# A transformer layer with a mixture of experts on one NeuronCore: first pair's slots freed in halves, the further block behind the eighth pair, bfloat16 one-hots, and the ninth weight unit behind the first gather

## The reference

```python
x = x + g1 * mix                                  # mix = [pooling | linear attention] @ w_out
h = rms_norm(x) * (1.0 + sc2) + sh2               # (512, 1024)
s = sigmoid(h @ w_router)                         # 32 experts in 4 groups of 8
# best group by the sum of its two best (s + bias); two best experts in it; gw = their s, normalised
for each token, for its two experts e:
    y += gw * ((silu(h @ w1[e]) * (h @ w3[e])) @ w2[e])      # w1, w3: 1024 x 512; w2: 512 x 1024
x = x + g2 * y
return rms_norm(x) * final_g
```

## Time and profile before

| | |
|---|---|
| median of 3 runs | 756.38 us (755.04 to 759.0) |
| the profiled execution, own time | 761.83 us |
| its span | 760.0 us |
| PE busy (matmuls) | 700.8 us, 92% |
| DVE, ACT, POOL busy | 343.1, 174.9, 55.5 us |
| transferred | 259.42 MB, mean 341 GB/s |
| chain that ended last | PE 75%, DMA 16%, DVE 7% |

### The profile page before, as it was taken

One profiled execution on the slowest core, in us unless ns is written; L12 is line 12 of the kernel. 1 busy time (PEld: TensorE's weight loads), 2 busy tenths in 40 slices (PEclk: granted clock), 3 DMA queues, 4 the chain that ended last, 5 costly groups with the idle time before them and its releaser, 6 DMA issues.

```text
span 760.0 us, 9258 instructions
## 1 busy us (share of the span) xinstructions
PE 700.8 (92%) x3822; PEld 388.3 (51%) x3822; DVE 343.1 (45%) x624; ACT 174.9 (23%) x309; POOL 55.5 (7%) x55
## 2 busy tenths in 40 slices
PE   3799999999898799989779999999999999998893
PEld 2578778777687444443424443443443443453442
DVE  3554988698865213323314233333333333332326
ACT  4332376532232020210110101110110110110104
POOL 2007700100000100000000000000000000000000
PEclk9899999999999899999987999999999999999997
DMA  9995353844738389998996999999999999999962
GB/s 337 388 382 202 139 200 132 314 147 206 292 137 347 131 354 427 426 425 326 430 425 281 420 415 427 426 426 426 426 428 427 426 427 428 425 428 427 429 286 110
DMA packets 38922, 259.42 MB, mean 341 GB/s; under 512 B 4126, under 2 KB 4510, under 8 KB 26208
## 3 DMA queue, kind: packets, MB, share of 16 engines
q1 hardware_dynamic: 34416, 250.11, 80.5%
q0 software_dynamic: 2688, 4.88, 1.7%
q10 hardware_dynamic: 1776, 3.84, 1.3%
HBM read 259.20 MB, written 4.19 MB: 347 GB/s over the span
## 4 chain that ended last, share of the span: by engine, by line
PE 75%; DMA 16%; DVE 7%; issue 1%; ACT 1%; SPq 1%; DVEq 0%; POOLq 0%
PE bank L904 26%; PE bank L611 16%; PE bank L913 12%; DMA ring<-in_w 8%; PE bank L921 4%; PE bank L922 3%; DMA ring<-in_w_in 3%; DMA xg_rows<-x_rows,keep 3%; DMA x_rows<-mid 2%; PE bank L878 2%; PE bank L893 2%; PE bank L929 1%; PE bank L896 1%; PE bank L731 1%; PE bank L886 1%
## 5 line engine op out<-in xcount | busy, mean ns | idle before, releaser
L904 PE MATMUL bank<-ring,low 128*64 128x512 f32 x944 | 229.7, 603 | 4.8 <-DMA ring<-in_w 4.0
L904 PEld LDWEIGHTS bank<-ring,low 128*64 128x64 f32 x944 | 74.4, 139 | 127.4 <-issue 127.4
L1678 DVE TENSOR_TENSOR x<-x,bank 128x512 f32<-128x512 f32 x136 | 84.4, 683 | 78.5 <-PE bank L922 76.7
L913 PE MATMUL bank<-ring,low 128*64 128x512 f32 x432 | 115.0, 600 | 0.9 <-DVE x L1678 0.9
L913 PEld LDWEIGHTS bank<-ring,low 128*64 128x64 f32 x432 | 35.6, 138 | 67.5 <-issue 65.9
L1668 DVE SCALAR_TENSOR_TENSOR y_raw<-bank,keep,g2b 128x512 f32<-128x512 f32 x32 | 24.0, 751 | 89.2 <-PE bank L913 89.2
L1735 DVE TENSOR_TENSOR low<-low,bank 128x512 f32<-128x512 f32 x16 | 11.0, 688 | 112.9 <-PE bank L904 112.9
L921 PE MATMUL bank<-y_hi,slot_tok 128*128 128x512 f32 x128 | 53.7, 420 | 0.2 <-DVE y_lo L1673 0.2
L922 PE MATMUL bank<-y_lo,slot_tok 128*128 128x512 f32 x128 | 50.6, 395 | 0.0
L1311 ACT COPY low<-bank 128x512 f32<-128x512 f32 x16 | 9.4, 586 | 173.6 <-PE bank L886 173.6
L1835 POOL DMA_INDIRECT xg_rows<-x_rows,keep x17 | 16.9, 996 | 432.5 <-PE bank L878 400.6
(11 more groups left out here) (248 smaller groups left out, 926.0 us busy)
## 6 DMA issues: line engine op xcount, KB each, us to landing
ring<-in_w SPq DMA_DIRECT2D x88, 2048.0 KB, 18.9
ring<-in_w_mod SPq DMA_DIRECT2D x11, 2048.0 KB, 12.3
mid<-in_w SPq DMA_DIRECT2D x11, 2048.0 KB, 17.9
ring<-in_w_in SPq DMA_DIRECT2D x4, 2048.0 KB, 21.7
ring<-in_w_out SPq DMA_DIRECT2D x2, 2048.0 KB, 10.2
x<-in_x SPq DMA_DIRECT2D x4, 512.0 KB, 6.1
mid<-in_w_mod SPq DMA_DIRECT2D x1, 2048.0 KB, 21.7
x_rows<-mid ACTq DMA_DIRECT2D x4, 512.0 KB, 13.7
```

What stands on the lines that cost most here:

```text
L904: last = mm(bk[e * CAP:(e + 1) * CAP, :], xb[:, k, e * CAP:(e + 1) * CAP], unit(n % SLOTS, KD)[:, k, :], start=k == 0, stop=k == KD - 1)
L913: last = mm(bk[e * CAP:(e + 1) * CAP, :], hid_t[:, k, e * CAP:(e + 1) * CAP], unit(n % SLOTS, KF)[:, k, hf * 512:(hf + 1) * 512], start=k ...
L1678: return v.tensor_tensor(acc[:, t, c], acc[:, t, c], bk[:, :], ALU.add)
```

## The change

1. `XPAIR` goes from 3 to 7: the further block stands behind the eighth pair.
2. Units 9 to 12, which follow the first pair's w1 and w3, are loaded as two halves of 1 MB each. A new semaphore, `a_half`, rises once the first half of the first pair's w1 (then w3) product has read rows 0 to 3 of the eight; the second half waits for `a_done` as before.
3. Unit 8's load also waits for the first gather's landing.
4. `mb10` and `mb11` stand behind `wo11`, on DVE the three `mod_steps` behind the left half's residuals, and the two reads of `mb10`, `mb11` behind the second `normed`.
5. The one-hot matrix is bfloat16; the routing weight goes in as three bfloat16 parts and the token number as two (five columns in the place of two), summed again after the product. ACT makes a bfloat16 identity. DVE makes the three parts for all experts at once, with five instructions between the count of tokens and the first one-hot.

```diff
-XPAIR = 3
+XPAIR = 7
...
-        + [f"wo0{t}" for t in range(NT)] + ["mb10", "mb11", "wo10", "wo11", "wo12", "hT00", "hT01", "wo13"]
+        + [f"wo0{t}" for t in range(NT)] + ["wo10", "wo11", "mb10", "mb11", "wo12", "hT00", "hT01", "wo13"]
...
+        onehot = place("onehot", LOW, [P, NT, P], BF16)
+        ident_b = place("ident_b", LOW + 256, [P, P], BF16)
...
+        HALVED = range(SLOTS, SLOTS + 4)
...
+            def expert_unit(n, half=None):
...
+                r = slice(0, kk) if half is None else slice(half * kk // 2, (half + 1) * kk // 2)
+                sp.dma_start(unit(slot, kk)[:, r, :], w[:, e, r, :]).then_inc(landed[slot], 16)
...
                     sp.wait_ge(job_done, JOB["hT31"] + 1)
                     sp.wait_ge(h2_saved, 16 * NT)
+                    sp.wait_ge(gath, 16)
...
-            for n in range(SLOTS, len(UNITS)):
+            for w_ in range(2):
+                for half, used in ((0, a_half), (1, a_done)):
+                    sp.wait_ge(used, w_ + 1)
+                    for e in range(2):
+                        expert_unit(HALVED[2 * w_ + e], half)
+            for n in range(SLOTS + 4, len(UNITS)):
...
                     for t in range(NT):
-                        mm(A1[e * CAP:(e + 1) * CAP, 0:2], onehot[:, t, e * CAP:(e + 1) * CAP],
+                        mm(A1[e * CAP:(e + 1) * CAP, 0:5], onehot[:, t, e * CAP:(e + 1) * CAP],
                            pair_cols[:, t, e, :], start=t == 0, stop=t == NT - 1)
                 for t in range(NT):
-                    last = nc.tensor.transpose(CA[:, t * P:(t + 1) * P], onehot[:, t, :], ident)
+                    last = nc.tensor.transpose(slots_bank[:, t * P:(t + 1) * P], onehot[:, t, :], ident_b[:, :])
...
                 for k in range(KD):
+                    if k == KD // 2 and n0 == 0:
+                        last.then_inc(a_half, 1)
...
-            mod_steps(6 * KD - 3, 6 * KD)
...
             for t in range(NT):
                 residual(0, t)
-            mod_row(10)
-            mod_row(11)
+            mod_steps(6 * KD - 3, 6 * KD)
...
             normed(1)
+            mod_row(10)
+            mod_row(11)
...
+            for i in range(3):
+                link(v.tensor_copy(w_parts[:, :, 0:E_N, i], weights))
+                if i < 2:
+                    link(v.tensor_tensor(weights, weights, w_parts[:, :, 0:E_N, i], ALU.subtract))
...
-                v.tensor_copy(w_slot[:, buf:buf + 1], A1[:, 0:1])
-                return v.tensor_scalar(row_of[:, buf:buf + 1], A1[:, 1:2], float(S), None, ALU.add)
+                v.tensor_reduce(w_slot[:, buf:buf + 1], A1[:, 0:3], AX_X, ALU.add)
+                return v.tensor_scalar(row_of[:, buf:buf + 1], A1[:, 3:4], A1[:, 4:5], float(S), ALU.add, ALU.add)
```

More of the change, by code:

```diff
@@ L160 @@
               + [f"mb{i}" for i in range(4, 10)] + [f"rb{h}" for h in range(HEADS)]
-              + [f"wo0{t}" for t in range(NT)] + ["mb10", "mb11"] + [f"wo1{t}" for t in range(NT)] + ["rk", "cnt"])
+              + [f"wo0{t}" for t in range(NT)] + ["wo10", "wo11", "mb10", "mb11", "wo12", "wo13", "rk", "cnt"])
 assert sorted(OUT_SCALAR + OUT_VECTOR) == sorted(JOBS)
@@ L196, in build @@
         big = place("big", BIG, [P, UNIT])
-        keep = place("keep", YA + 3 * D, [P, 965])
+        keep = place("keep", YA + 3 * D, [P, 976])
         h_hi = place("h_hi", BIG, [P, KD, S], F32R)
@@ L237, in take, with place_kept @@
             at[0] += n
-            assert at[0] <= 965
+            assert at[0] <= 976
             return keep[:, at[0] - n:at[0]]
+        def place_kept(name, shape):
+            return place(name, YA + 3 * D + (at[0] + 7) // 8 * 8, shape, BF16)
         cp = take(CP_N)
@@ L404, in build @@
         w2_r = A["w2"][0].rearrange("e (p k) n -> p e k n", p=P)
+        HALVED = range(SLOTS, SLOTS + 4)
         def landed_at(n):
             slot = n % SLOTS
-            return 16 * (PRE_USES[slot] + len([m for m in range(slot, n + 1, SLOTS) if UNITS[m][0] is not None]))
+            loads = [2 if m in HALVED else 1 for m in range(slot, n + 1, SLOTS) if UNITS[m][0] is not None]
+            return 16 * (PRE_USES[slot] + sum(loads))
         def full(eng, name):
@@ L469, in expert_unit @@
                 w, kk = ((w1_r, KD), (w3_r, KD), (w2_r, KF))[k // 2]
-                sp.dma_start(unit(slot, kk), w[:, e, :, :]).then_inc(landed[slot], 16)
+                r = slice(0, kk) if half is None else slice(half * kk // 2, (half + 1) * kk // 2)
+                sp.dma_start(unit(slot, kk)[:, r, :], w[:, e, r, :]).then_inc(landed[slot], 16)
             for n in (3, 6, 2, 0, 7, 1, 4, 5, 8):
@@ L831, in _ @@
             second_half(1)
+            summed_rows(10)
+            summed_rows(11)
             second_half(2)
@@ L1585, in _ @@
             dve.wait_ge(keep_in, 48)
+            row_in_tile = tok[:, 0:1].unsqueeze(2).to_broadcast([P, NT, 2])
+            link(v.tensor_scalar(pair_cols[:, :, :, 3], row_in_tile, float(S), None, ALU.add))
+            v.tensor_tensor(pair_cols[:, :, :, 4], tok.unsqueeze(2).to_broadcast([P, NT, 2]), pair_cols[:, :, :, 3], ALU.subtract)
             read_out(dve, "lg")
@@ L1623, in _ @@
             link(v.reciprocal(rt_m, rt_m))
-            v.tensor_tensor(gwt[:, :, 0:E_N], gwt[:, :, 0:E_N], rt_m.unsqueeze(2).to_broadcast([P, NT, E_N]), ALU.mult)
-            dve.wait_ge(ident_in, 16)
-            v.tensor_copy(pair_cols[:, :, :, 1], tok.unsqueeze(2).to_broadcast([P, NT, 2]))
+            weights = gwt[:, :, 0:E_N]
+            link(v.tensor_tensor(weights, weights, rt_m.unsqueeze(2).to_broadcast([P, NT, E_N]), ALU.mult))
             b = full(dve, "rk")
@@ L1643, in one_hot @@
                 v.tensor_scalar(rank_pair, ranks, off, None, ALU.add).then_inc(cols_ready, 1)
-                v.tensor_copy(pair_cols[:, :, :, 0], weights)
+                v.tensor_copy(pair_cols[:, :, :, 0:3], weights)
                 dve.wait_ge(cols_ready, cols_count)
-                return v.tensor_tensor(onehot_t[:, :, :].rearrange("p t (e s) -> p (t e) s", e=2),
+                return v.tensor_tensor(onehot[:, :, :].rearrange("p t (e s) -> p (t e) s", e=2),
                                        rank_pair.rearrange("p t e -> p (t e)").unsqueeze(2).to_broadcast([P, NT * 2, CAP]),
```

24 lines of the change are left out of this document (13 added, 11 removed).

## The result

| | before | changed |
|---|---|---|
| median of the runs | 755.75 us (755.04 to 759.0, 4 runs) | 737.45 us (736.52 to 739.79, 4 runs) |
| ratio | | 0.9754, interval 0.9717 to 0.9792 |
| the profiled execution, own time | 761.83 us | 737.88 us |
| its span | 760.0 us | 736.0 us |

The change is 2.5% faster. The time lies in the range of the prediction, 5.7 us above its forecast of 731.8.

The account below looks back on a forecast made before the run. The weight stream plus a fixed tail was taken to bind, PE finishing 4.5 us earlier. Stream -14.8 - 9.8 = -24.6 us turned 761.83 into 737.2; less 5.45 to the median gave 731.8 us, range 725 to 741.

Parts of the forecast that it names:

- first gather issued, landed: Before the first pair: with unit 8 held back, the gather takes the shortest time, 3.3 us, and lands at 247.2.
- last filler ends: PE before the first pair's turn: the last filler, 4.75 us, ends at 247.0, together with the gather.
- holes around the further block: Weight stream at 342 to 350 and 410 to 416 us: 4.4 and 5.4 us lost; both vanish, -9.8 us.
- stream in all: Weight stream: 14.8 us from the earlier start plus 9.8 us from the holes, -24.6 us together.
- three rivals (736, 737 and 739): Start comes later, about 736, chance 0.15; slow halves, 737, 0.06; PE binds because one-hots save nothing, 739, 0.05.
- a clock under 1.00 in the filler: Sign on PE before the first pair: a filler clock below 1.00 would show the prediction wrong.
- where over 415 was named: Sign in the weight stream: above 415 GB/s in every stretch from 254 us to the last weights.
- The rival in which they are slow: Units 9 to 12: the half loads don't hide their beginnings and ends; 742 at most, nearer 737; chance 0.06.
- it has not been idle, so I take the high clock: PE turning the first pair's rows: high clock assumed, 0.9 us in place of 1.97.
- the start comes later: Around the first one-hot: idle PE's clock falls, filler 2 to 4 us longer, or gather takes 10.7; about 736; chance 0.15.
- the same step leads to 731.8: Whole kernel: the median lies 5.45 us below the profiled execution's time; applied to 737.2, this gives 731.8.
- the lead in the prediction: Further block: behind the eighth pair PE has gained 14.4 us against 12.7 needed; holes vanish with 1.7 us to spare.

Follow-up runs that it names:

- Experiment 6: Changed kernel without the product of y's low part in the pairs' combinations, so PE has less work; 738.09 us, ratio 0.9742 to before.
- experiment 7: Changed kernel with 21 instead of 7 filler transposes ahead of the first one-hot; 739.04 us, ratio 0.9747 to before.
- 9: Changed kernel with the last pair's w3 and w2 loads also in halves and 20 fillers instead of seven; 737.04 us, ratio 0.9708 to before.
- 5: Kernel before with parts 1 to 4 of the change, one-hots left in float32; 744.8 us, ratio 0.98 to before.
- 11: Kernel before, unchanged, run once more as the second copy; 754.79 us, span 753.0.
- 10: Kernel before, unchanged, run once more as the first copy; 756.84 us, span 754.7.

## Why the prediction was right, and where it was off

| step, as the prediction put it | forecast | measured |
|---|---|---|
| `wo13` earlier | 5.0 us | 5.2 |
| spread sums reached, and covered | 204.3 | 204.50, no wait |
| first gather issued, landed | 243.9, 247.2 | 242.8, unit 8 issued at 247.28 |
| weight parts on DVE | 1.5 us | 1.6 (237.26 to 238.84) |
| one-hot matmuls, saved each pair | 0.8 | 0.84 |
| last filler ends | 247.0 | 248.8 |
| first product begins | 248.8 | 250.47 |
| first half issued | 252.3 | 254.15 |
| holes around the further block | gone | gone |
| stream in all | -24.6 | -23.95 |
| own time of the profiled execution | 737.2 | 737.88 |
| own time to median | -5.45 | -0.43 |

**What bounds the kernel was read rightly.** Experiment 6 takes 15.8 us more of waiting into PE and moves the end by 0.5. PE's chain was put 4.5 us ahead of the weights; it waits 5.4. The terms show in single runs, by the start of the last w1 product and less what stood before the edit's place: the further block 9.6 us (forecast 9.8), halves 2.9, the gather's wait 4.4, the order of the sums 5.6. They are terms of the stream and add up to 22.5, with the result at 24.0. The one-hots' 6.8 in span is on PE's own chain, and doesn't add to them.

**What met by luck.** The sum of 24.6 against 23.95 hides two misses of opposite sign: the start gained 13.7 us and not 14.8, and the rest, the holes, 10.3 and not 9.8. The first gather landed when the forecast said, but it was issued 1.1 us earlier and took 4.4 us, where I had taken the shortest of all gathers, 3.3. And 737.45 lies outside 728 to 734, where the forecast had its 0.57; it is close to the prices of three rivals (736, 737 and 739), of which one happened, and that at 1.2 us instead of some 4. Of the signs, a clock under 1.00 in the filler was named as one of being wrong, and it came; and in the halves' stretches 280, 399 and 380 GB/s stand where over 415 was named. One small slip: of the 1.40 us of matmuls a pair, 12 at 0.04 leave 0.9 to save at best, not 0.95.

**The halves.** The rival in which they are slow fell, and so did the estimate worked out from the Trainium skill's table ("DMA: Bandwidth & Descriptors", section Bandwidth), by which they would have cost 5 us. The 1 MB loads run at 421 GB/s in 260 to 275, and with whole units the stream is 2.9 us later, not earlier. The table's row is for a transfer issued from POOL; here the halves are issued from SP and queued behind each other. Which of the two makes the difference was not tested. Only in 252 to 256, where unit 8 has ended and the first half goes out at 254.15, is the rate 280.

**The start, 1.7 us late.** The step that failed is the last filler at its old 4.75 us, together with "it has not been idle, so I take the high clock". The turn itself did run at the high clock (0.88 us). But PE was idle for 1.56 us before the one-hot, the filler of seven matmuls ahead of it lasted only 0.98, and the clock was 0.50 in 240 to 244. The rival "the start comes later" named this place and this mechanism and priced it at 2 to 4 us; it happened, at 1.2 us, and in experiments 7 and 9 more filler in the place of the idle time kept the clock up. The idle time isn't needed for the fall, as experiments 5 and 11 show. The remaining 0.5 us is there before the last filler begins (242.87, where the sum has 247.0 - 4.75 = 242.25); 0.3 of it is the second one-hot's matmuls at the fallen clock (0.93 against 0.64 us in experiment 7).

**The step that cost 5 us of forecast: "the same step leads to 731.8".** I took the 5.45 us between the profiled execution and the median as something that lies on every execution of this program alike, and carried it over. Experiments 10 and 11 show what it was: a half clock behind idle times in the third pair (1.96 us, where the further block's slots are prepared) and in the further block (3.00 us), which made PE late, which held SP, which opened the hole at 410 to 416. That hole is in the sum already, as 5.4 of the 9.8 us. The start of the last pair's w1 product, which waits for its weights in all of them, shows it: 716.98 in the long execution, 710.77 and 709.14 in the copies, 693.05 with the change. Less the start of the stream (267.82, 267.90 and 265.82 against 254.15), the rest, the holes, was worth 23.9 - 13.7 = 10.3 us in the long execution, and 17.7 - 13.7 = 4.0 and 16.1 - 11.7 = 4.4 in the short ones. So the sum was right against the long execution (24.6, measured 24.0), and then I subtracted nearly the same microseconds once more. A forecast from a short execution would have come out right: by the prediction's own formula the first copy's holes are 2.8 us (278 GB/s in 342 to 350) and 1.6 (381 in 400 to 416), and 756.84 - 14.8 - 4.4 = 737.6; the second's are 2.6 (284) and 1.4 (387), its stream starts 2.0 us earlier, and 754.79 - 12.8 - 4.0 = 738.0. Measured: 737.45.

The trace had a sign of this. The earlier trace rows show the clock at 0.57 behind one idle time of 1.96 us and at 1.00 behind another, and I used the row for a rival and not for the question of why this execution was the longest of those shown. The Trainium skill ("TensorE: Matmul & The Clock Gate", Part 1) says that the number of slow matmuls at a kernel's start varies from run to run. The copies show the same far from the start: same instructions, same idle times (1.96 us before L893 in both), 0.57 in one and 1.00 in the other. Why it falls in one execution and not in the next stays open.

This would also explain, with the mean clocks above, why the runs of before lie between 753.5 and 763.9 us in the later comparisons, and those of the changed kernel only between 736.5 and 741.1. With the further block behind the eighth pair PE's clock still falls (0.78 in 480 to 500), but the stream runs on at 425 GB/s: I take it that SP has a free place by then, as the lead in the prediction says. That is read from profiled executions; of the others only time and mean clock are known.

## What to carry to other kernels

A profiled execution that is longer than the median is not the median plus a constant: find out in which stretch it is long before the step to the median is taken, above all when the change removes that very stretch. If a queue with few places feeds a stream, work that holds a place belongs where the consumer has most in hand; here the stream ended 9.6 us earlier with the further block behind the eighth pair instead of the fourth, in executions whose clock fell around it, and by the two copies of before some 4 us of that remain where it doesn't fall. A slot may be given back in parts: here loads of 1 MB, queued behind each other, ran at 421 GB/s beside 424 to 427 for 2 MB, and the earlier start was worth 2.9 us. And take the same row of several executions before an edit of 1 us is judged by its span: here the clock of one product near the end moved it by 0.9.

## What was not expected of the hardware

- One program's clock parts between executions at the same instruction: 0.57 against 1.00 in 337.4 to 341.4, 0.53 against 1.00 in 400 to 410, and the other way round in the routing, where the profile before and the first copy stand at 1.00 and the second copy at 0.50 (245 to 249):

```profile
245.00:249.00 4.00, 3.94 (x32) 3.53 (x31) 1.03 (x5) 0.59 (x1) 0.58 (x1) 0.50 0.27 65
```

- Two stretches at half clock, about 4 and 10 us long and 350 us and more ahead of the end, made PE 6.4 us late, which came to 5.3 us of span, because they held the weight queue.
- Fourteen more matmuls whose result nobody reads (2.51 us for all 21 instead of 0.98 for seven) made the 42 behind them 1.2 us faster, in both executions that had such a filler.
- A gather of 128 rows takes 8.09 us beside a 2 MB load and 4.34 without it.
